# Expert weights in 16 KB rows, two ring slots to a matrix, on one core of a Trainium2 chip

## The chip, the cores and the metric

The kernel runs on one core of a Trainium2 chip (trn2). The metric is the device time of one execution, in microseconds (us). The kernel before takes 2732.53 us, the median of 3 runs (2731.9 to 2733.25).

## The reference: what is computed

A float32 network over 256 tokens of 1024 features. Its first part has two layers. Each layer scales and shifts its input by vectors made from a condition (the `ada` weights), mixes along the sequence (a gated convolution), adds and normalises, and runs a mixture of experts. Two more layers follow (`f1`, `hy`, `f2` in the kernel: feed-forward, attention, feed-forward), which the change does not touch. What matters here, from the reference:

```
def expert_block(args):
    xblk, e = args
    hid = jax.nn.silu(xblk @ w_gate[e]) * (xblk @ w_up[e])
    return hid @ w_down[e]
```

There are 32 experts to a layer. `w_gate[e]` and `w_up[e]` are 1024 x 512 and `w_down[e]` is 512 x 1024, so an expert has three matrices of 2 MB and a layer 192 MB, in float32. Each token goes to two experts of one group, by a router's scores.

## The kernel before, in words

**The ring.** All weights come through one ring in SBUF: `ring`, of `NSLOT` = 6 slots, each 128 partitions x 2048 float32 (8 KB to a partition, 1 MB in all). `wanted` lists what is needed in the order of use; from it the planner makes `pieces`, one to a slot: piece n goes to slot n % 6. `sync_engine` walks over the pieces in order, on the one queue of SP. Before it issues piece n it waits until piece n - 6 has been read (semaphore `ring_read`, line L734), then it issues the DMA at L738. The order of TensorE's steps is written out by hand in `moe`.

**An expert's pieces.** `want_experts` asks for four `up` pieces of expert e (gate and up weights of input features 0 to 511, then gate and up weights of 512 to 1023) and then for the two `down` pieces of expert e - 1 (inner features 0 to 255, then 256 to 511). That is six pieces, so each kind comes back to the same slots every time. Within a piece, partition p holds 4 whole rows of the gate or up matrix (input features 4p to 4p + 3 of that half), or 2 rows of the down matrix, side by side in memory: one run of 8 KB to a partition.

**TensorE in the stage of the experts.** For each e it runs `up(e)`, `down(e - 1)`, every second time `combine`, then `turn(e)` and, for the first 24, `gather` of later tokens. `up(e)` (matmul at L1096) has up to 64 gathered tokens as the stationary operand, 128 x 64, and the weights as the moving operand; the token block takes half of the array's columns, and so the inner features are cut in two halves c: c = 0 goes to PSUM partitions 0 to 63, c = 1 to 64 to 127, and both run beside each other. One matmul has 512 moving columns: 256 gate weights and 256 up weights of the same half and input chunk, from two neighbouring slots:

```
r4 = two.rearrange("p u (k n) -> p k u n", k=4)
ins = pe.matmul(b[64 * c:64 * c + 64, :], xg[:, u, kc, x0:x0 + CAP], r4[:, k, :, 256 * c:256 * c + 256],
                start=kc == 0, stop=kc == KC - 1)
```

There are 16 such matmuls to an expert in the program. A float32 matmul appears in the profile as two instructions, so an expert has 32 of them there. After the first 8 (the first half of the input features) two slots are given back, after the second 8 the next two. `down(e)` (L1115) has 8 matmuls and gives back one slot after each half.

**After `up`.** ScalarE takes silu of the gate half of the bank (L2491) and VectorE multiplies by the up half (L1961). Both use `by_two`, so that neighbouring inner features come apart (stride of two elements), because partition p of a down piece holds features 2p and 2p + 1. `turn` transposes the product for `down`.

**Around it.** `router_shift` (L804) moves the scale and shift columns of `ab` to the feature order that the gathered tokens have (4p + k within a half), by 16 small matmuls with `ident[:, k::4]` as the stationary operand. ScalarE copies the result (L2465). The tokens' high and low parts `vh` and `vl` are written by L2473 (ScalarE) and L1827 (VectorE) through `by_four`, which reads `vv` with a stride of four elements, 16 bytes. The gather evacuations L1931, L1940, L2453 and L2461 use the scale. For expert 0 the first half of gate and up and both down pieces are read early to places outside the ring (`early_loads`, L709).

## Time and profile before

| | |
|---|---|
| median of 3 runs | 2732.53 us |
| the profiled execution's own time | 2728.11 us |
| its span in the trace | 2726.3 us |
| mean granted TensorE clock | 0.983 of 2.4 GHz |
| TensorE matmuls busy | 2486.4 us, 91% |
| TensorE weight loads busy | 1839.1 us, 67% |
| VectorE, ScalarE, GpSimd busy | 1291.5, 863.6, 298.5 us |
| read from HBM | 709.72 MB, 261 GB/s over the span |
| DMA packets | 254197 |

Busy time is a union over the span: two matmuls that run beside each other count once. The duration of one instruction (mean ns) is then longer than busy time divided by count. The share of DMA is the mean over the core's 16 DMA engines; a stretch that is full reads 1.00 or 1.01.

### The profile page before, as it was taken

Reading aid. Unit: us, or ns where it says so; the run is one execution under the profiler, and the core shown is the slowest. Engines: PE = TensorE matmul, PEld = TensorE weight load, DVE = VectorE, ACT = ScalarE, POOL = GpSimd, SP = SyncE. Lnnn points to the kernel's source line nnn. Section 1 sums busy time; section 2 is a strip of 40 time slices with the busy share of each in tenths; the row PEclk is TensorE's granted clock in tenths of the full one; section 3 lists DMA queues with packets and bytes.
Section 4 is the critical chain, followed back from the end, with each engine's and each line's share of the span. In section 5 each row is a group of like instructions: output and inputs, shape, how many; then the busy total and the mean of one; then the engine's idle time right before and its main releaser. Section 6 shows DMA issues by size and latency. Waiting matters only on the chain.

```text
span 2726.3 us, 39201 instructions
## 1 busy us (share of the span) xinstructions
PE 2486.4 (91%) x15956; PEld 1839.1 (67%) x15957; DVE 1291.5 (47%) x2250; ACT 863.6 (32%) x1462; POOL 298.5 (11%) x382
## 2 busy tenths in 40 slices
PE   5899898988898988988899999989999999989998
PEld 3564433333694333333599888879989988888997
DVE  5454323221664332222454675565465467555545
ACT  2242111110332111110244444444444444444443
POOL 0210010000000010000000122330010011233001
PEclk9999999999998999999999999999999999999999
DMA  9988999999764999999765443335655544334372
GB/s 354 366 357 318 420 420 419 415 420 419 265 238 175 420 419 419 416 420 419 294 202 186 132 150 124 124 124 182 201 167 199 194 137 155 117 116 155 128 241 81
DMA packets 254197, 716.26 MB, mean 263 GB/s; under 512 B 14544, under 2 KB 171872, under 8 KB 197696
## 3 DMA queue, kind: packets, MB, share of 16 engines
q1 hardware_dynamic: 250336, 708.80, 69.0%
q0 software_dynamic: 1616, 2.45, 0.3%
q8 instruction: 129, 2.11, 0.3%
q10 hardware_dynamic: 2064, 2.47, 0.3%
q14 instruction: 52, 0.43, 0.0%
HBM read 709.72 MB, written 1.05 MB: 261 GB/s over the span
## 4 chain that ended last, share of the span: by engine, by line
PE 59%; DMA 22%; issue 7%; DVE 6%; POOL 3%; ACT 2%; SPq 1%; ACTq 0%; DVEq 0%; POOLq 0%
DMA ring<-in_e_w_up_dram 20%; PE w L837 17%; PE w L1096 10%; PE y L879 10%; PE w L841 9%; PE w L1115 2%; DMA ring<-in_ada_w_dram 2%; PE w L1372 2%; PE y L762 1%; POOL arena L2770 1%; PE w L1357 1%; PE y L1148 1%; DVE wsp L1481 1%; DMA xa<-in_x_dram 1%; SPq L738 1%
## 5 line engine op out<-in xcount | busy, mean ns | idle before, releaser
L1481 DVE TENSOR_TENSOR wsp<-ring,wsp 128x1024 fp32r<-128x1024 f32 x470 | 578.7, 1237 | 406.0 <-ACT wsp L1471 405.3
L837 PE MATMUL w<-hh,wsp 128*128 128x256 f32 x4832 | 638.4, 285 | 8.5 <-DVE wsp L1481 8.1
L837 PEld LDWEIGHTS w<-hh,wsp 128*128 128x128 f32 x4832 | 607.6, 192 | 28.9 <-issue 15.9
L1471 ACT CAST wsp<-ring 128x1024 fp32r<-128x1024 f32 x470 | 487.9, 1045 | 398.2 <-PE w L841 217.5
L1096 PE MATMUL w<-ring,arena 128*64 128x512 f32 x2016 | 459.8, 598 | 104.8 <-DMA ring<-in_e_w_up_dram 98.3
L1096 PEld LDWEIGHTS w<-ring,arena 128*64 128x64 f32 x2016 | 155.5, 137 | 374.6 <-issue 373.5
L841 PE MATMUL w<-hl,wsp 128*128 128x256 f32 x2416 | 339.1, 283 | 0.0
L841 PEld LDWEIGHTS w<-hl,wsp 128*128 128x128 f32 x2416 | 311.8, 192 | 0.0
L879 PE MATMUL y<-wsp,zsp 128*128 128x512 f32 x1104 | 267.2, 392 | 3.9 <-DVE wsp L1481 3.8
L2491 ACT ACTIVATE ht<-w 128x256 f32<-128x256 f32 x64 | 40.0, 625 | 700.4 <-PE w L1096 700.4
L1961 DVE TENSOR_TENSOR ht<-w,ht 128x256 f32<-128x256 f32 x64 | 39.5, 618 | 455.1 <-ACT ht L2491 455.1
L879 PEld LDWEIGHTS y<-wsp,zsp 128*128 128x128 f32 x1104 | 201.8, 188 | 44.5 <-DVE wsp L1481 6.1
L1115 PE MATMUL w<-ring,ht 128*64 128x512 f32 x992 | 225.1, 592 | 1.1 <-issue 1.1
L1115 PEld LDWEIGHTS w<-ring,ht 128*64 128x64 f32 x992 | 82.5, 137 | 130.7 <-issue 101.6
L1974 DVE TENSOR_TENSOR arena<-w,gb 64x512 f32<-64x512 f32 x128 | 88.2, 689 | 144.1 <-PE w L1115 142.1
L2696 POOL TENSOR_TENSOR zsp<-arena,zsp 128x256 fp32r<-128x256 f32 x92 | 69.2, 752 | 724.8 <-ACT zsp L2347 724.8
L2683 POOL TENSOR_TENSOR small<-small 128x1 f32<-128x1 f32 x20 | 16.2, 812 | 817.5 <-DVE small L1611 817.5
L2770 POOL TENSOR_SCALAR arena<-arena,small 128x128 f32<-128x128 f32 x96 | 62.1, 665 | 275.0 <-DVE small L2251 275.0
L2540 ACT ACTIVATE arena<-w 128x256 f32<-128x256 f32 x88 | 33.8, 384 | 144.9 <-PE w L841 144.9
L762 PE MATMUL y<-ring,arena 128*32 128x512 f32 x384 | 53.9, 679 | 22.6 <-DMA ring<-in_ada_w_dram 22.5
L879 PE MATMUL y<-wsp,hh 128*128 128x512 f32 x224 | 69.8, 393 | 4.9 <-DVE wsp L1481 3.4
L2080 DVE TENSOR_TENSOR arena<-w,arena 128x256 f32<-128x256 f32 x88 | 37.4, 425 | 77.8 <-ACT arena L2540 77.6
(341 smaller groups left out, 2478.3 us busy)
## 6 DMA issues: line engine op xcount, KB each, us to landing
ring<-in_e_w_gate_dram SPq DMA_DIRECT2D x126, 1024.0 KB, 8.6
ring<-in_e_w_up_dram SPq DMA_DIRECT2D x126, 1024.0 KB, 10.8
ring<-in_e_w_down_dram SPq DMA_DIRECT2D x124, 1024.0 KB, 12.2
ring<-in_ffn_in_dram SPq DMA_DIRECT2D x88, 1024.0 KB, 5.4
ring<-in_w_in_dram SPq DMA_DIRECT2D x50, 1024.0 KB, 5.2
ring<-in_ada_w_dram SPq DMA_DIRECT2D x48, 1024.0 KB, 12.6
ring<-in_ffn_out_dram SPq DMA_DIRECT2D x44, 1024.0 KB, 5.0
ring<-in_b_w_in_dram SPq DMA_DIRECT2D x12, 1024.0 KB, 8.9
```

Of the source, the lines that this page charges most:

```text
L762: ins = pe.matmul(ada_sum(l, cb)[32 * g:32 * g + 32, :], cact[:, kc, :], ring[:, n % NSLOT, g * 512:(g + 1) * 512], start=kc == 0, stop=kc ...
L837: pe.matmul(dst, a[:, kc * m:(kc + 1) * m], hh[:, kc, :], start=kc == 0 and j == 0, stop=False)
L841: ins = pe.matmul(dst, wh[:, kc * m:(kc + 1) * m], hl[:, kc, :], start=False, stop=kc == KC - 1)
L879: ins = pe.matmul(YB[2 * t + h][:, :], z[:, t * P:(t + 1) * P], a[:, h * 512:(h + 1) * 512], start=k == 0 and j == 0, stop=k == n - 1 and ...
L1096: ins = pe.matmul(b[64 * c:64 * c + 64, :], xg[:, u, kc, x0:x0 + CAP], r4[:, k, :, 256 * c:256 * c + 256], start=kc == 0, stop=kc == KC - 1)
L1115: ins = pe.matmul(b[64 * dh:64 * dh + 64, :], he[:, i, c, h, :], w[:, c, 512 * dh:512 * dh + 512], start=h == 0 and c == 0, stop=h == 1 an ...
L1372: ins = pe.matmul(b[:, T * c:T * c + T], a[:, k * 256 + c * P:k * 256 + c * P + P], z[:, k, :], start=k == 0 and j == 0, stop=k == 3 and j ...
L1471: ac.copy(shaped(halves(i)[0], u.shape), u.cut(ring[:, u.piece % NSLOT, :])).then_inc(*mark("w_high", i))
L1481: ve.tensor_tensor(shaped(lo, u.shape), u.cut(ring[:, u.piece % NSLOT, :]), shaped(hi, u.shape).bitcast(F32), ALU.subtract).then_inc(*mark ...
L1974: ve.tensor_tensor(ye[p0:p0 + 64, pr, dh, :], b[at_, :], gb[at_, 512 * dh:512 * dh + 512], ALU.mult).then_inc(*mark("ye", l, d_))
L2696: po.tensor_tensor(lo, src, hi.bitcast(F32), ALU.subtract).then_inc(*mark("z_lo", key, k))
L2770: ins = po.tensor_scalar(sm[:, 2 * u + q, a:z], sm[:, 2 * u + q, a:z], rd[:, k:k + 1], 0.5, ALU.mult, ALU.mult)
```

## The change

Gate, up and down matrices now come whole. A gate or up matrix is one DMA of 2 MB (`wide_piece`), partition p getting its 8 rows 8p to 8p + 7, 16 KB in one run, in two neighbouring slots; a down matrix likewise, 4 rows of 4 KB to a partition. Order: gate, up, then down of the expert before. Exceptions: expert 0's gate and up stay cut in two (rows 0 to 3 of each partition early, 4 to 7 through the ring, and the ring's half is now used first), and down of expert 31 stays in two pieces.

`up(e)` reads the gate matrix through first and gives its two slots back, then the up matrix. A matmul has 256 moving columns instead of 512, and there are 32 instead of 16. Inner feature 4q + 2c + j goes to half c, place j, q: the moving operand of a matmul is now read through `by_part`, with a step of four elements (16 bytes) between columns. The silu and the product need no `by_two` any more. A down matrix's two slots are given back together, after the second half of `down`.

For the new order of the input features (8p + k) `router_shift` gets 32 small matmuls instead of 16, with `twice` (two copies of the identity, made by VectorE) as its source; each writes both of two neighbouring features, and GpSimd picks one by a mask (two TENSOR_SCALAR and one TENSOR_TENSOR, 128 x 16) before the gather evacuations may run. `by_eight` reads `vv` with a stride of eight elements.

The diff, cut to its core:

```
@@ constants
+    for u in range(2):
+        c[:, C_ODD + u] = np.arange(P) // 16 % 2 == u
@@ want_experts
-                    wanted.extend(("up", l, e_, h) for h in range(4))
+                    wanted.extend(("up", l, e_, u) for u in range(2))
                 if e_ >= 1:
-                    wanted.extend(("down", l, e_ - 1, h) for h in range(2))
+                    wanted.append(("down", l, e_ - 1))
@@ pieces
+        def wide_piece(key, src):
+            n = len(pieces)
+            assert n % 2 == 0
+            piece_of[key] = n
+            pieces.append({"wide": src, "units": [], "read": n})
+            pieces.append({"units": [], "read": n})
...
-                src = I[("e_w_gate", "e_w_up")[u]][l, e_, 512 * g:512 * g + 512, :]
+                src = I[("e_w_gate", "e_w_up")[u]][l, e_].rearrange("(p k) n -> p k n", p=P)
...
-        def in_ring(key):
-            return ring[:, piece_of[key] % NSLOT, :]
+        def two_slots(s, k):
+            return ring[:, s:s + 2, :].rearrange("p u (k n) -> p (u k) n", k=k // 2)
...
-        def by_four(a):
-            return a.rearrange("p (g q k) -> p g k q", g=2, k=4)
+        def by_eight(a):
+            return a.rearrange("p (q k) -> p k q", k=KC)
-        def by_two(a):
-            return a.rearrange("p (q c) -> p q c", c=2)
+        def by_part(a):
+            return a.rearrange("p (q c j) -> p c j q", c=2, j=2)
@@ sync_engine
+                if "wide" in piece:
+                    slot_free(n - NSLOT)
+                    slot_free(n + 1 - NSLOT)
+                    sp.dma_start(two_slots(n % NSLOT, piece["wide"].shape[1]), piece["wide"]).then_inc(
+                        *mark(f"ring{n % NSLOT}", n, by=16))
@@ router_shift
-                o = WB[3][:, 64:80].rearrange("p (v g k) -> p v g k", v=2, g=2)
+                o = WB[3][:, 64:96].rearrange("p (v k b) -> p v k b", v=2, k=KC)
                 for j in range(4):
-                    for k in range(4):
-                        pe.matmul(o[32 * j:32 * j + 32, :, :, k], ident[:, k::4],
-                                  ab[:, 0:2, :].rearrange("p v (g j) -> p v g j", g=2)[:, :, :, j], start=True, stop=True)
+                    for k in range(KC):
+                        pe.matmul(o[32 * j:32 * j + 32, :, k, :], twice[:, k::KC],
+                                  ab[:, 0:2, 2 * j:2 * j + 2], start=True, stop=True)
@@ up(e_), e_ > 0
+                        for v in range(2):
+                            np_ = piece_of["up", l, e_, v]
+                            pe.wait_ge(*at(f"ring{np_ % NSLOT}", np_))
+                            w = two_slots(np_ % NSLOT, KC)
+                            for kc in range(KC):
+                                for c in range(2):
+                                    ins = pe.matmul(b[64 * c:64 * c + 64, T * v:T * v + T], x(kc), by_part(w[:, kc, :])[:, c],
+                                                    start=kc == 0, stop=kc == KC - 1)
                             ins.then_inc(*mark("ring_read", np_))
@@ vector_engine, the product
-                        ve.tensor_tensor(hd[:, i, :].rearrange("p (c q) -> p q c", c=2), by_two(b[:, T:2 * T]),
-                                         hd[:, i, :].rearrange("p (c q) -> p q c", c=2), ALU.mult).then_inc(*mark("hd", l, e_))
+                        ve.tensor_tensor(hd[:, i, :], b[:, T:2 * T], hd[:, i, :], ALU.mult).then_inc(*mark("hd", l, e_))
@@ scalar_engine, silu
-                        ac.activation(hd[:, i, :].rearrange("p (c q) -> p q c", c=2), by_two(bank_of(("up", e_))[:, 0:T]), ACT.Silu).then_inc(*mark("silu", l, e_))
+                        ac.activation(hd[:, i, :], bank_of(("up", e_))[:, 0:T], ACT.Silu).then_inc(*mark("silu", l, e_))
@@ pool_engine, moe
+                po.tensor_scalar(wide, cols[:, :, 0], const[:, C_ODD:C_ODD + 1], None, ALU.mult).then_inc(*mark("ones", "even", l))
+                po.tensor_scalar(odd_cols, cols[:, :, 1], const[:, C_ODD + 1:C_ODD + 2], None, ALU.mult).then_inc(*mark("ones", "odd", l))
+                po.wait_ge(*at("ones", "odd", l))
+                po.tensor_tensor(wide, wide, odd_cols, ALU.add).then_inc(*mark("ones", "scale", l))
```

How the instructions stand on SP's queue, in the middle of layer 0, where two short loads of norm vectors (`lnp`) stand between the down weights of one expert and the next expert's gate weights (each row: line, tensor written and read, shape; in brackets the semaphore it waits for). Before:

```order
L738 DMA ring<-in_e_w_down_dram 128x2048 [waits ring_read] x2
L725 DMA lnp<-in_ffn_ln_g_dram 128x1024 [waits x_new]
L725 DMA lnp<-in_ffn_ln_b_dram 128x1024
L738 DMA ring<-in_e_w_gate_dram 128x2048 [waits ring_read]
L738 DMA ring<-in_e_w_up_dram 128x2048 [waits ring_read]
L738 DMA ring<-in_e_w_gate_dram 128x2048 [waits ring_read]
L738 DMA ring<-in_e_w_up_dram 128x2048 [waits ring_read]
L738 DMA ring<-in_e_w_down_dram 128x2048 [waits ring_read] x2
```

And with the change:

```order
L754 DMA ring<-in_e_w_down_dram 128x4096 [waits ring_read]
L745 DMA lnp<-in_ffn_ln_g_dram 128x1024 [waits x_new]
L745 DMA lnp<-in_ffn_ln_b_dram 128x1024
L754 DMA ring<-in_e_w_gate_dram 128x4096 [waits ring_read]
L754 DMA ring<-in_e_w_up_dram 128x4096 [waits ring_read]
L754 DMA ring<-in_e_w_down_dram 128x4096 [waits ring_read]
```

Six DMAs of 1 MB to an expert have become three of 2 MB. The gate matrix stands whole ahead of the up matrix.

TensorE's queue for one expert, from its first weights to the transposes of `turn` (`w` is the PSUM bank, `arena` holds the gathered tokens, `ht` the inner features). Before:

```order
L1096 MATMUL w<-ring,arena 64x512 [waits ring1,ring0,ye]
L1096 MATMUL w<-ring,arena 64x512 x7
L1096 MATMUL w<-ring,arena 64x512 [waits ring3,ring2]
L1096 MATMUL w<-ring,arena 64x512 x7
L1115 MATMUL w<-ring,ht 64x512 [waits ring4,he]
L1115 MATMUL w<-ring,ht 64x512 x3
L1115 MATMUL w<-ring,ht 64x512 [waits ring5]
L1115 MATMUL w<-ring,ht 64x512 x3
```

And with the change:

```order
L1130 MATMUL w<-ring,arena 64x256 [waits ring0,ye]
L1130 MATMUL w<-ring,arena 64x256 x15
L1130 MATMUL w<-ring,arena 64x256 [waits ring2]
L1130 MATMUL w<-ring,arena 64x256 x15
L1149 MATMUL w<-ring,ht 64x512 [waits ring4,he]
L1149 MATMUL w<-ring,ht 64x512 x3
L1149 MATMUL w<-ring,ht 64x512 [waits ring4]
L1149 MATMUL w<-ring,ht 64x512 x3
```

The matmuls of `up` are twice as many and half as wide. They wait for one DMA at a time where they waited for two, of 2 MB in both cases. `down` keeps its matmuls, and both its halves wait for the same DMA.

## Rows read from the trace of the kernel before

**Rows 1.** The page's part 1: busy time, share of the span, instructions.
```profile
PE 2486.4 (91%) x15956; PEld 1839.1 (67%) x15957; DVE 1291.5 (47%) x2250; ACT 863.6 (32%) x1462; POOL 298.5 (11%) x382
```
**Rows 2.** Busy time by stretch; columns as in the first line; third stretch: feed-forward.
```profile
core 0: us, PE busy (x) PEld busy (x) DVE busy (x) ACT busy (x) POOL busy (x), PEclk, DMA share, GB/s
284.00:722.00 438.00, 379.65 (x1750) 168.87 (x1747) 123.85 (x208) 58.05 (x102) 11.42 (x7) 0.99 1.00 410
860.00:1325.00 465.00, 411.14 (x1888) 176.71 (x1884) 122.43 (x195) 52.94 (x90) 10.21 (x4) 1.00 1.01 416
1400.00:1500.00 100.00, 100.00 (x705) 94.11 (x705) 48.78 (x48) 45.72 (x61) 8.88 (x12) 1.00 0.67 223
```
**Rows 3.** The chain that ended last, two experts of layer 0: start, us, what.
```profile
599.92 3.67 PE w L1096 x16
603.60 0.33 SPq L738
603.98 10.78 DMA ring<-in_e_w_up_dram
614.88 3.67 PE w L1096 x16
```
**Rows 4.** Groups on TensorE: shapes, count, busy us, mean ns, idle before and releaser.
```profile
L1096 PE MATMUL w<-ring,arena 128*64 128x512 f32 x2016 | 459.8, 598 | 104.8 <-DMA ring<-in_e_w_up_dram 98.3 <-issue 3.2 <-DVE arena L1940 2.9
L1096 PE MATMUL w<-arena 128*64 128x512 f32 x32 | 7.3, 597 | 3.5 <-DVE arena L1931 3.5
L941 PE MATMUL w<-arena 128*32 128x256 f32 x144 | 8.8, 379 | 0.0
L837 PE MATMUL w<-hh,wsp 128*128 128x256 f32 x4800 | 634.0, 285 | 8.5 <-DVE wsp L1481 8.1 <-DVE vv L2196 0.4
```
**Rows 5.** SP's queue, one expert: start, us, DMA issued.
```profile
598.62 0.33 SPq L738 DMA_DIRECT2D ring<-in_e_w_gate_dram  x1
598.99 0.43 SPq L738 DMA_DIRECT2D ring<-in_e_w_up_dram  x1
603.60 0.33 SPq L738 DMA_DIRECT2D ring<-in_e_w_gate_dram  x1
603.98 0.43 SPq L738 DMA_DIRECT2D ring<-in_e_w_up_dram  x1
605.32 2.04 SPq L738 DMA_DIRECT2D ring<-in_e_w_down_dram  x2
613.79 0.33 SPq L738 DMA_DIRECT2D ring<-in_e_w_gate_dram  x1
```
**Rows 6.** Groups on ScalarE and VectorE, operands with and without a step.
```profile
L2509 ACT CAST hh<-arena 128x1024 fp32r<-128x1024 f32 x32 | 33.3, 1041 | 21.5 <-DVE arena L1974 21.5
L2473 ACT CAST zsp<-vv 128x1024 fp32r<-128x1024 f32 x4 | 8.2, 2048 | 0.0
L1481 DVE TENSOR_TENSOR wsp<-ring,wsp 128x1024 fp32r<-128x1024 f32 x468 | 577.2, 1239 | 406.0 <-ACT wsp L1471 405.3 <-issue 0.3
L1827 DVE TENSOR_TENSOR wsp<-vv,zsp 128x1024 fp32r<-128x1024 f32 x4 | 8.0, 1996 | 2.4 <-ACT zsp L2473 2.4
```
**Rows 7.** TensorE weight loads of 32 columns: ns min/median/max; contiguous, then stepped.
```profile
L762 PEld LDWEIGHTS y<-ring,arena x384: 106/110/177, 11.2 to 213.8; 128*32 128x32 f32 x192
L804 PEld LDWEIGHTS w<-ab,const x64: 134/156/158, 193.4 to 814.7; 128*32 128x32 f32 x64
```
**Rows 8.** Groups of silu and product, and the same without a step elsewhere.
```profile
L2491 ACT ACTIVATE ht<-w 128x256 f32<-128x256 f32 x64 | 40.0, 625 | 700.4 <-PE w L1096 700.4
L1961 DVE TENSOR_TENSOR ht<-w,ht 128x256 f32<-128x256 f32 x64 | 39.5, 618 | 455.1 <-ACT ht L2491 455.1
```
**Rows 9.** TensorE by time in layer 0, `router_shift`: start, us, instructions.
```profile
193.38 1.27 PE L804 MATMUL w<-ab,const 128*32 128x4 f32 x29
222.22 3.65 PE L1096 MATMUL w<-arena 128*64 128x512 f32 x16 [1.77 <-DVE arena L1931]
```

More of the change, by code:

```diff
@@ L39 @@
 NFIRST = 161
-NCONST = 2145
+C_ODD = 2145
+NCONST = 2147
 CAP = 64
@@ L313, in program @@
         var, rsd = small[:, 212:214], small[:, 214:216]
+        both_cols, odd_cols = small[:, 256:288], small[:, 288:304]
         uA = area(0, KC, 288)
@@ L565, in program @@
+                src = I[("e_w_gate", "e_w_up")[u]][l, e_].rearrange("(p k) n -> p k n", p=P)
+                assert e_ or len(pieces) % 2 == u
+                if e_ == 0:
+                    early[l].append((early_up[:, u, :], src[:, 0:4, :], "in_x"))
+                    piece_of[w] = len(pieces)
+                    pieces.append({"parts": [(lambda r: r, src[:, 4:8, :])], "units": [], "read": len(pieces) + 1 - u})
+                else:
+                    wide_piece(w, src)
             elif w[0] == "down":
-                _, l, e_, h = w
@@ L696, in late, with slot_free @@
                                     sp.sem_inc(s_, 1)
+            def slot_free(n):
+                if pieces[n]["units"]:
+                    for i in pieces[n]["units"]:
+                        sp.wait_ge(*low_done(i))
+                else:
+                    sp.wait_ge(*at("ring_read", pieces[n].get("read", n)))
             def early_loads(l):
@@ new lines, in up @@
+                    if e_ == 0:
+                        for v in range(2):
+                            np_ = piece_of["up", l, 0, v]
+                            pe.wait_ge(*at(f"ring{np_ % NSLOT}", np_))
+                        s0 = np_ % NSLOT - 1
+                        for h, two in ((1, ring[:, s0:s0 + 2, :]), (0, early_up)):
+                            if h == 0:
+                                pe.wait_ge(*at("in_x", "early", l))
+                            r4 = two.rearrange("p u (k q c j) -> p k c u j q", k=4, c=2, j=2)
+                            for k in range(4):
+                                for c in range(2):
+                                    o = b[64 * c:64 * c + 64, :].rearrange("p (u j q) -> p u j q", u=2, j=2)
+                                    ins = pe.matmul(o, x(4 * h + k), r4[:, k, c], start=(h, k) == (1, 0), stop=(h, k) == (0, 3))
+                            ins.then_inc(*(mark("ring_read", np_) if h else mark("ring_read", "early_up", l)))
+                    else:
+                        for v in range(2):
+                            np_ = piece_of["up", l, e_, v]
+                            pe.wait_ge(*at(f"ring{np_ % NSLOT}", np_))
+                            w = two_slots(np_ % NSLOT, KC)
+                            for kc in range(KC):
+                                for c in range(2):
+                                    ins = pe.matmul(b[64 * c:64 * c + 64, T * v:T * v + T], x(kc), by_part(w[:, kc, :])[:, c],
+                                                    start=kc == 0, stop=kc == KC - 1)
@@ L1111, in down @@
                             pe.wait_ge(*at(f"ring{np_ % NSLOT}", np_))
-                            w = ring[:, np_ % NSLOT, :].rearrange("p (k n) -> p k n", k=2)
-                        for c in range(2):
+                            s0 = (piece_of["down", l, e_, 0] + h) % NSLOT
+                            w = ring[:, s0, :].rearrange("p (k n) -> p k n", k=2)
+                        for j in range(2):
                             for dh in range(2):
-                                ins = pe.matmul(b[64 * dh:64 * dh + 64, :], he[:, i, c, h, :], w[:, c, 512 * dh:512 * dh + 512],
-                                                start=h == 0 and c == 0, stop=h == 1 and c == 1)
-                        if e_:
+                                ins = pe.matmul(b[64 * dh:64 * dh + 64, :], he[:, i, j, h, :], w[:, j, 512 * dh:512 * dh + 512],
+                                                start=h == 0 and j == 0, stop=h == 1 and j == 1)
+                        if e_ and (h == 1 or np_ != piece_of["down", l, e_, 1]):
                             ins.then_inc(*mark("ring_read", np_))
@@ L1928, in gathered_half @@
                     ve.wait_ge(*at("route_s", "row", l))
+                    ve.wait_ge(*at("ones", "scale", l))
                     for k in range(2):
@@ L2450, in gathered_half @@
                     ac.wait_ge(*at("route_s", "row", l))
+                    ac.wait_ge(*at("ones", "scale", l))
                     for k in range(2):
```

128 lines of the change are left out of this document (57 added, 71 removed).

## The prediction
> **What bounds the kernel now.** I began with the page's first part. TensorE is busy for 2486.4 of 2726.3 us [rows 1], but that is a mean over stages with different limits, so I read the stretches of the two layers' experts, the only ones the change touches in size. There the 16 DMA engines are full, share 1.00 and 1.01 at 410 and 416 GB/s, while TensorE is busy for 379.65 of 438 and 411.14 of 465 us, 87 and 88% [rows 2]. So these 903 us are bound by the transfers, and TensorE has some 12% to spare. The chain of waits shows one beat of this: 3.67 us of matmuls, 0.4 us on SP's queue, 10.78 us until the up weights have landed, and again; 614.88 - 599.92 = 14.96 us from expert to expert [rows 3]. An expert's weights are 6.29 MB, and 6.29 MB in 14.96 us are 420 GB/s. The reader should see that the 10.78 us is no latency but a queue: six transfers are out or in line at a time.
>
> TensorE's own cost of an expert: 14.96 x 0.88 = 13.1 us. Of it `up` takes (459.8 + 7.3) / 64 = 7.3 us [rows 4]. It waited 104.8 us ahead of `up` in all, nearly all of it for the up weights [rows 4]. That idle time is the whole cover for anything that makes matmuls dearer; past it, each microsecond counts in full.
>
> **The change, part by part.**
>
> *Rows of 16 KB.* 184 DMAs of 2 MB replace 368 of 1 MB (62 gate and up matrices and 30 down matrices to a layer). No row has a 16 KB transfer, so its price is bounded. Nothing gained is one end. For the other I estimate a fixed cost per row from two stretches: the experts' 8 KB rows move at 416/1.01 = 412 GB/s per unit of share, the feed-forward stretch, by the source's shapes two thirds 1 KB rows and one third 4 KB rows, at 223/0.67 = 333 [rows 2]. On 16 engines an 8 KB row then takes 318 ns, and 1 MB of the mixture 50.4 us of engine time; with a cost a per row and b per KB that solves to a of about 15 ns, b of about 38 ns. A 16 KB row would take 621 ns instead of 636, 2.4% off, at most 22 us of the 903. I take the middle, 11 us, for the case in which the transfers stay the bound.
>
> The Trainium skill (DMA: Bandwidth & Descriptors, Where 436 GB/s comes from) puts the fabric's ceiling at 435 GB/s. The same page's table (Measured) gives 341 GB/s for a DMA of 1 MB and 425 for 16 MB, by which doubling the DMA's size should pay a lot; the trace disagrees, 420 GB/s with 1 MB, since the queue is never empty. By the ceiling alone the gain would be at most 3.5% of 903, 31 us.
>
> *Twice as many matmuls, half as wide.* The streaming work is the same. What is added is the cost of one more pair. Where four column groups run beside each other at 256 columns, an instruction takes 8800/144 = 61 ns of busy time, a set of four 245 ns [rows 4], against 213 ns that 256 columns need at the pace of `up` (427 of its 2 x 228 = 456 ns for 512 columns; 427 is 512 columns at two cycles of 2.4 GHz). So 32 ns are overhead. An expert has 32 pairs now: 32 x 245 = 7.8 us, half a microsecond more, 35 us in all. As long as it is only this, it lies within the 104.8 us of idle time and costs nothing.
>
> *The moving operand with a step of 16 bytes.* Here I see the decision. Before, a matmul of `up` reads runs of 256 neighbouring weights. Now every column lies 16 bytes from the one before. No matmul of the kernel before has such a moving operand of any length, so this too is bounded by its neighbours. The lower end is nothing. Against it stand three engines' readers in this very trace. ScalarE casts 128 x 1024 in 1041 ns from neighbouring elements and in 2048 ns where it reads `vv` with a step of 16 bytes; VectorE's subtraction goes from 1239 to 1996 ns on the same operand [rows 6]. And TensorE's other operand: a weight load of 32 columns takes 106 ns at least without a step and 134 at least (156 at the median) with `ident[:, k::4]`, a step of 16 bytes [rows 7]. Per element that is +0.98, +0.74, and +0.88 ns (+1.44 at the medians). A matmul of `up` takes 427/512 = 0.83 ns for a column, so such a reader would about double it. What speaks for nothing: a float32 column stays in the array for two cycles, and at 256 columns the single-pass matmuls take 634.0/4800 us = 132 ns each, so the moving reader delivers at least 1.9 elements per ns from neighbouring addresses [rows 4], more than `up` asks of it per half. But there it passes over 16 bytes in 2 ns; with the step it would have to pass over 16 bytes in every 0.83 ns, faster than ScalarE (2048/1024 = 2 ns), VectorE or the weight loads do in their rows. I take the doubling.
>
> The Trainium skill (Advanced Engine Details and Errata, Memory Cachelines) says that SBUF has lines of 16 bytes and that at least two hits on a line are needed to hide the access, with a penalty otherwise. By that rule the step taken here, one hit to a line, is just past what is free. It speaks of engines in general and gives no factor; rows 6 agree with it for ScalarE and VectorE, and no row shows it for a moving operand.
>
> The sum: 64 experts x 32 pairs = 2048 pairs, each 2 x 213 + 32 = 459 ns, 940 us, for 467 us now: +473 us. The 104.8 us of idle time go: +368 us. An expert then takes 5.7 us longer, the transfers have a share near 0.7, and their rate no longer matters.
>
> *Slots.* Gate slots come back after half of `up`, up slots after the other half, as before. Both down slots now come back at the end of `down`, where the first came back some 1.8 us earlier. The queue covers it: the down DMAs are issued at 605.3 and 607.0, when the 2 MB issued at 603.6 and most of those of 598.6 are still in line (they land at 614.8), and nothing else is issued until 613.8 [rows 3, 5]. Zero.
>
> *Silu and product* lose their steps and perhaps 0.2 us each of 625 and 618 ns [rows 8]; TensorE runs `down(e - 1)` meanwhile. Zero.
>
> *`router_shift`* has 32 more instructions a layer at 1270/29 = 44 ns [rows 9], 1.4 us, 2.8 in all. GpSimd's three small operations (under a microsecond each) and VectorE's copy run while the router works, between 194 and 222 us [rows 9]: covered; without cover some 3 us a layer. I count +2.8 us.
>
> Sum: 2728.1 + 368 + 2.8 = 3099 us against the profiled execution's own time. The median of the runs is 4.4 us above that: **3104 us**. With +0.74 ns a column instead (VectorE's) a pair takes 435 ns, and the time is 3055; with +0.98 (ScalarE's) it is 3180; that case's own range is 3045 to 3230.
>
> **The rivals.**
>
> *The step is free.* The moving operand is read as fast as before, TensorE goes from 13.1 to 13.6 us an expert and the transfers stay the bound at 14.6 to 14.96. Then the time is 2732.5 - 11 + 2.8 = 2724 us, 2705 at best. For it: the moving reader is the fastest of all in rows 4, and it may fetch ahead. Against it: rows 6 and 7. This is the case on the other side.
>
> *Free, and no gain.* The 16 KB rows are cut into smaller packets, so the change doesn't do what it says, or the fixed cost per row is nil. 2730 to 2738 us. A packet count that has not fallen would show it.
>
> *Both halves share one reader.* The two matmuls of a pair then share the slowed rate: 4 x 213 + 32 = 884 ns a pair, 1810 us of `up`, +1343 - 105 + 3: 3974 us. Against it: four column groups stream 256 columns each in 245 ns [rows 4], so they are not served in turn now.
>
> *The queue runs dry behind the down slots.* It decides once less than 1.8 us of transfers are in line as `down` ends; 62 x 1.8 = +112 us, 2845. Rows 3 and 5 show over 7 us in line.
>
> **How the numbers follow.** The doubled read 0.51; free and gaining 0.32; free with nothing gained 0.08; the shared reader 0.05; the dry queue and other mishaps 0.04. Of the doubled case a little lies above 3230. Low end 2703, near the best of the free case, high end 3230: it leaves out the shared reader and the doubled case's upper tail, some 0.13. Cases of both signs hold most of the chance, so note that 3045 to 3230 is the likeliest one's range and that the middle between is nearly empty. 0.2% is about what a measurement of this kernel can tell from no change. Faster 0.32, the same 0.08, slower 0.60.
>
> **What would show it.** The group of `up`'s matmuls on TensorE: instructions of 256 columns with a mean well above the 379 ns of rows 4, and a busy time near 940 us rather than 500. DMA share in the experts near 0.7, not 1.0; no idle time ahead of `up` released by a transfer. The chain of waits there all TensorE. 23552 fewer packets, if rows are moved as 16 KB. If the group's busy time is below some 570 us, the central step is wrong and the time must come from the DMA rate: then 2705 to 2730 us, and GB/s above 416.

## The result, and the profile after

| | before | changed |
|---|---|---|
| median of the runs | 2732.89 us (2731.9 to 2733.51, 4 runs) | 3113.21 us (3108.41 to 3120.01, 4 runs) |
| span of the profiled execution | 2726.3 us | 3105.8 us |
| TensorE busy | 2486.4 us, 91% | 2966.9 us, 96% |
| `up` on TensorE, all groups | 467.1 us | 941.1 us |
| idle time ahead of `up` in the ring | 104.8 us | 8.0 us |
| share of the DMA engines in layer 0's experts | 1.00 | 0.79 |
| packets on SP's queue | 250336 | 223840 |

The changed kernel takes 1.140 times as long, 95% interval 1.1385 to 1.1414. Slower, as forecast: 3104 us were predicted, within 2703 to 3230.

The same view as [rows 1], from the page of the changed kernel (busy time, share of the span, instructions of each engine):

```profile
PE 2966.9 (96%) x18004; PEld 2007.1 (65%) x18005; DVE 1280.2 (41%) x2252; ACT 848.6 (27%) x1462; POOL 302.0 (10%) x388
```

TensorE gains 480.5 us of busy time, and the span grows by 379.5. The first stretch of [rows 2], layer 0's experts, of the changed kernel (same columns: busy time and instructions of PE, PEld, DVE, ACT, POOL; granted clock; DMA share; GB/s):

```profile
284.00:722.00 438.00, 434.96 (x1962) 177.02 (x1960) 86.22 (x146) 35.65 (x68) 10.43 (x4) 1.00 0.79 302
```

The two bounds have changed places. Before, the transfers had a share of 1.00 and TensorE 87%; now TensorE has 99% and the transfers 0.79, at 302 GB/s instead of 410. The granted clock was 1.00 in the stretch, the 2.4 GHz level, and 0.99 before, so the extra time does not come from the clock.

TensorE's groups after, to set beside [rows 4] (shapes, count, busy us, mean ns, idle before and its releaser; L1130 is `up` from the ring; L1121 are its early parts of expert 0, and L1149 is `down`):

```profile
L1130 PE MATMUL w<-ring,arena 128*64 128x256 f32 x3968 | 911.5, 632 | 8.0 <-issue 8.0
L1149 PE MATMUL w<-ring,ht 128*64 128x512 f32 x992 | 224.8, 594 | 1.1 <-issue 1.1
L1121 PE MATMUL w<-arena 128*64 128x512 f32 x32 | 14.8, 1078 | 0.0
L1121 PE MATMUL w<-ring,arena 128*64 128x512 f32 x32 | 14.8, 1078 | 3.5 <-DVE arena L1971 3.5
```

`up` costs 911.5 + 14.8 + 14.8 = 941.1 us for the same multiplications that took 467.1, and no transfer releases any of it any more. `down`, whose operand kept its neighbours, takes 594 ns a matmul, 592 before. L1121 is the cleanest row: instructions of 512 columns as before, 597 ns before, 1078 now. What differs is the order in which the moving operand is read.

The chain that ended last, for one expert and a part of the next, as in [rows 3] (start us, us, what):

```profile
608.25 14.63 PE w L1130 x64
622.89 3.44 PE w L1149 x16
626.32 0.37 PE w L1161 x2
626.69 0.17 PE w L1170 x2
626.86 0.50 PE w L1172 x4
627.36 0.94 PE w L1095 x4
628.30 14.63 PE w L1130 x64
```

From this expert to the next it is now 628.30 - 608.25 = 20.05 us, where the expert of [rows 3] took 14.96, and TensorE holds every link. The 10.78 us wait for the up weights has gone from the chain. The 64 instructions are 32 pairs, one instruction for each half: 14.63 us by 32 is 457 ns a pair.

Silu and product, beside [rows 8], got shorter by 240 and 193 ns, on engines that wait for TensorE anyway (same columns as [rows 8]):

```profile
L2001 DVE TENSOR_TENSOR ht<-w,ht 128x256 f32<-128x256 f32 x64 | 27.2, 425 | 814.8 <-ACT ht L2530 814.8
L2530 ACT ACTIVATE ht<-w 128x256 f32<-128x256 f32 x64 | 24.6, 385 | 1082.7 <-PE w L1130 1053.2
```

### The profile page after: what moved, and what is told of

It is laid out like the page before. It is cut to its first block, busy times and chain, and to the rows that moved or that the text cites. A ratio compares the mean times of both kernels' runs of the same rounds, so it can differ in the third digit from the quotient of the medians.

```text
span 3105.8 us, 43240 instructions
## 1 busy us (share of the span) xinstructions
PE 2966.9 (96%) x18004; PEld 2007.1 (65%) x18005; DVE 1280.2 (41%) x2252; ACT 848.6 (27%) x1462; POOL 302.0 (10%) x388
## 3 DMA queue, kind: packets, MB, share of 16 engines
q1 hardware_dynamic: 223840, 708.79, 62.7%
## 4 chain that ended last, share of the span: by engine, by line
PE 84%; issue 5%; DVE 4%; DMA 2%; POOL 2%; ACT 2%; ACTq 0%; SPq 0%; DVEq 0%; POOLq 0%
PE w L1130 29%; PE w L862 16%; PE y L904 9%; PE w L866 8%; PE w L1149 7%; PE y L1182 2%; DMA ring<-in_ada_w_dram 1%; PE w L1095 1%; PE w L1407 1%; PE w L1121 1%; PE y L787 1%; PE w L1392 1%; POOL arena L2817 1%; DVE wsp L1516 1%; DMA xa<-in_x_dram 1%
## 5 line engine op out<-in xcount | busy, mean ns | idle before, releaser
L1130 PE MATMUL w<-ring,arena 128*64 128x256 f32 x3968 | 911.5, 632 | 8.0 <-issue 8.0
L1130 PEld LDWEIGHTS w<-ring,arena 128*64 128x64 f32 x3968 | 322.0, 154 | 558.2 <-issue 556.3
L2001 DVE TENSOR_TENSOR ht<-w,ht 128x256 f32<-128x256 f32 x64 | 27.2, 425 | 814.8 <-ACT ht L2530 814.8
L2530 ACT ACTIVATE ht<-w 128x256 f32<-128x256 f32 x64 | 24.6, 385 | 1082.7 <-PE w L1130 1053.2
L1149 PE MATMUL w<-ring,ht 128*64 128x512 f32 x992 | 224.8, 594 | 1.1 <-issue 1.1
L1149 PEld LDWEIGHTS w<-ring,ht 128*64 128x64 f32 x992 | 75.1, 141 | 140.8 <-issue 140.8
L1407 PE MATMUL w<-zsp,wsp 128*128 128x256 f32 x576 | 71.5, 284 | 3.0 <-DVE zsp L2250 3.0
L1407 PEld LDWEIGHTS w<-zsp,wsp 128*128 128x128 f32 x576 | 69.6, 192 | 6.2 <-issue 6.2
```

Source lines behind the costliest of these rows:

```text
L1130: ins = pe.matmul(b[64 * c:64 * c + 64, T * v:T * v + T], x(kc), by_part(w[:, kc, :])[:, c], start=kc == 0, stop=kc == KC - 1)
L1149: ins = pe.matmul(b[64 * dh:64 * dh + 64, :], he[:, i, j, h, :], w[:, j, 512 * dh:512 * dh + 512], start=h == 0 and j == 0, stop=h == 1 an ...
L1407: ins = pe.matmul(b[:, T * c:T * c + T], a[:, k * 256 + c * P:k * 256 + c * P + P], z[:, k, :], start=k == 0 and j == 0, stop=k == 3 and j ...
```

## The experiments

Ratios are to the kernel before, run beside each version on the same chip. Where one run alone was made, no interval is given. "A pair" is always two instructions of 256 columns in the profile, one for each half; its price is the group's busy time by half the count (where the instructions have 512 columns, half of that again). a, b, j and so on are the versions by the first letter of their labels.

### Is it the step? The same kernel, neighbouring columns

```diff
@@ up(e_), after
-    ins = pe.matmul(b[64 * c:64 * c + 64, T * v:T * v + T], x(kc), by_part(w[:, kc, :])[:, c],
+    ins = pe.matmul(b[64 * c:64 * c + 64, T * v:T * v + T], x(kc), w[:, kc, T * c:T * c + T],
```

(and the same for expert 0's early part).

> The changed kernel, but each matmul of `up` reads 256 neighbouring weights (features 256c to 256c + 255 for half c) instead of every fourth; the inner features then meet the wrong rows of the down matrix, all else is the change's. Theory 1 (the 16-byte step is the cost): the matmuls of `up` fall from 911 us busy to 470 to 500 us (pairs of about 245 ns), the transfers bound the experts again, 2710 to 2735 us. Rival (twice as many, narrower matmuls and their weight loads, or the new slot order, are the cost): 911 us busy stays, about 3110 us. The same run shows what 16 KB rows are worth: DMA at 420 GB/s if nothing (2733 to 2738 us), up to 430 if a fixed cost per row is saved (2710 to 2722 us).

Measured: 2748.62 us (2742.27 to 2756.37, 4 runs), 1.0074 times before, 1.0053 to 1.0094. The groups of `up` and of `down` on TensorE, columns as above:

```profile
L1130 PE MATMUL w<-ring,arena 128*64 128x256 f32 x3968 | 451.9, 382 | 38.6 <-DMA ring<-in_e_w_up_dram 27.3 <-issue 6.1 <-DMA ring<-in_e_w_gate_dram 5.1
L1149 PE MATMUL w<-ring,ht 128*64 128x512 f32 x992 | 226.2, 596 | 64.7 <-DMA ring<-in_e_w_down_dram 63.5 <-issue 1.1
```

911.5 us become 451.9, and the time falls by 365 us. Nearly all of the loss was the step. The size of the rest was not as expected: `up` is below the 470 to 500 us, the time above the 2710 to 2735. Two things stand out. A pair costs 451.9/1984 = 228 ns, exactly half of the 456 ns of the 512-column pair: cutting the matmuls in two costs nothing. And the kernel is still 0.7% slower than before; TensorE now waits most for **down** weights, 63.5 us, where before it waited for up weights.

### The step alone, in the kernel before

```diff
@@ up(e_), before
-    ins = pe.matmul(b[64 * c:64 * c + 64, :], xg[:, u, kc, x0:x0 + CAP], r4[:, k, :, 256 * c:256 * c + 256],
+    ins = pe.matmul(b[64 * c:64 * c + 64, :].rearrange("p (u j q) -> p u j q", u=2, j=2), xg[:, u, kc, x0:x0 + CAP],
+                    r4[:, k].rearrange("p u (q c j) -> p c u j q", c=2, j=2)[:, c],
```

> The kernel before with one edit: its matmuls of `up` (512 columns, 8 KB rows, old order of pieces) read each half's columns with the change's 16-byte step; the inner features meet the wrong rows of the down matrix. Theory 1: 1024 pairs of 2 x 427 + 32 ns, about 900 us busy for 460 now, less the idle time it uses up: 3070 to 3110 us. Rival (narrow matmuls, slot order): `up` stays at 460 us busy and the time at 2733 us.

Measured: 3101.6 us, one run. The group of `up` from the ring:

```profile
L1096 PE MATMUL w<-ring,arena 128*64 128x512 f32 x2016 | 920.5, 1080 | 8.0 <-issue 8.0
```

With 8 KB rows, wide matmuls, the old slots and the old shift, the step by itself brings 372 us (the kernel before, beside it, took 2729.99 us). 920.5/1008 = 913 ns a pair of 512 columns, 457 for 256. So the parts do not have to come together: one of them does it.

### Keeping the change's order of features, with a step of two elements inside

```diff
@@ by_part, and the order of the output
-            return a.rearrange("p (q c j) -> p c j q", c=2, j=2)
+            return a.rearrange("p (q c j) -> p c q j", c=2, j=2)
@@ silu and product read and write through by_two again, as before
```

The moving operand now reads two neighbours and skips two: both halves of every 16 bytes are used.

> The change, but the moving operand takes features 4q + 2c and 4q + 2c + 1 one after the other: two neighbours (8 bytes), then 8 bytes left out; silu and product put them apart as in the kernel before. Same result as the reference. If the price hangs on 16 bytes being passed over for each single column (about 1.67 ns for 16 bytes), two columns to 16 bytes take the 0.83 ns each that float32 needs anyway: `up` 470 to 500 us busy, 2710 to 2735 us. If every gap between addresses costs, `up` lies between 600 and 911 us busy and the time between 2800 and 3110 us.

Measured: 2747.46 us (2746.02 to 2749.13, 4 runs), 1.0058 times before, 1.0041 to 1.0075. TensorE's groups:

```profile
L1134 PE MATMUL w<-ring,arena 128*64 128x256 f32 x3968 | 472.5, 391 | 36.1 <-DMA ring<-in_e_w_up_dram 23.4 <-DMA ring<-in_e_w_gate_dram 6.6 <-issue 6.1
L1153 PE MATMUL w<-ring,ht 128*64 128x512 f32 x992 | 226.2, 596 | 51.3 <-DMA ring<-in_e_w_down_dram 50.0 <-issue 1.1
```

238 ns a pair. It recovers 366 of the 380 us with the change's layout in memory; the 2710 to 2735 us expected were missed, as in a. The feature order that the down weights want was never the trouble; the order in which a matmul walks through it was.

### How the price depends on the step

```diff
@@ up(e_), before, 8 bytes
-    r4[:, k, :, 256 * c:256 * c + 256],
+    r4[:, k, :, c::2],
@@ up(e_), after, 12 bytes (::3), and in another kernel 32 bytes (::8)
-    by_part(w[:, kc, :])[:, c],
+    flat[:, min(kc * 512 + c, 2 * SLOT - 3 * (T - 1) - 1):][:, ::3][:, 0:T],
```

> The kernel before, its matmuls of `up` reading every second weight (step 8 bytes, features 2q + c; wrong ones for the down matrix). Two columns come from each 16 bytes at 0.83 ns a column, 16 bytes in 1.67 ns. If pairs were free because of that and not because the two were neighbours: 460 us busy, 2733 us. If only real neighbours are free: 600 us busy or more, 2780 us or more.

> The changed kernel with the moving operand of `up` (experts 1 to 31) read with a step of 3 elements, 12 bytes, from the same two slots; the columns are then not the right ones. If the price is set by how fast 16 bytes are passed over, a column costs 12/16 of the stepped one: with 1.78 ns for a column at 16 bytes (457 ns for 256), 1.34 ns, 343 ns a pair, some 680 us busy for 3968 instructions and a time of 2850 to 2880 us. If a column is free as long as its step is below 16 bytes: 450 to 480 us busy and about 2745 us. If any step costs as 16 bytes do: 911 us busy, 3110 us.

> The same with a step of 8 elements, 32 bytes. If a column's price is one access to memory however far the next is (what I expect), nothing changes against 16 bytes: 911 us busy, about 3110 us. If it grows with the distance: about 1820 us busy, time about 4000 us.

Measured, one run each (the kernel before beside them, one run too: 2738.8 us): 2734.37, 2883.88 and 3110.95 us. Each is the first case of its expectation, 12 bytes 4 us above its range. One line of TensorE's groups from each, first the kernel before with 8 bytes, then the changed kernel with 12, then with 32:

```profile
L1096 PE MATMUL w<-ring,arena 128*64 128x512 f32 x2016 | 484.2, 623 | 86.5 <-DMA ring<-in_e_w_up_dram 80.4 <-issue 6.1
```

```profile
L1130 PE MATMUL w<-ring,arena 128*64 128x256 f32 x3968 | 691.8, 513 | 8.6 <-issue 7.0 <-DVE arena L1980 1.0 <-DMA ring<-in_e_w_gate_dram 0.6
```

```profile
L1130 PE MATMUL w<-ring,arena 128*64 128x256 f32 x3968 | 925.6, 640 | 8.0 <-issue 8.0
```

| step | columns to 16 bytes | ns a pair of 256 | ns a column |
|---|---|---|---|
| 4 bytes (neighbours) | 4 | 228 | 0.89 |
| pairs, 16 bytes apart | 2 | 238 | 0.93 |
| 8 bytes | 2 | 240 | 0.94 |
| 12 bytes | 1.33 | 349 | 1.36 |
| 16 bytes | 1 | 457 to 459 | 1.79 |
| 32 bytes | 1 | 467 | 1.82 |

The price follows how many stretches of 16 bytes the operand goes through, and does not grow with the distance. At 12 bytes 256 columns go through 192 of them: 349/192 = 1.82 ns each; at 16 and 32 bytes through 256, 1.79 and 1.82 ns each. At 8 bytes it is 128, 1.8 x 128 = 230 ns, about what the columns take anyway, so the step is nearly free. Steps above 32 bytes and other types than float32 were not run. The Trainium skill (Advanced Engine Details and Errata, Memory Cachelines) wants at least two hits on a line of 16 bytes; for this moving operand the table agrees at both sides of that limit, 240 ns with two hits and 457 with one.

In the kernel before, a step of 8 bytes is hidden: the group is 24.4 us dearer than in [rows 4] and the idle time ahead of it falls from 104.8 to 86.5 us. The cover worked as read from [rows 4].

### Do the two halves share a reader?

```diff
@@ up(e_), after: the halves one after the other
-    for kc in range(KC):
-        for c in range(2):
+    for c in range(2):
+        for kc in range(KC):
```

and the same with neighbouring columns.

> The change, with the loop over the two halves c outside the loop over input chunks: 8 matmuls of one half, then 8 of the other, so that two matmuls that could run beside each other are no longer neighbours. Theory 1a (each stream is slowed to half its rate, both still run beside each other in the changed kernel): an instruction now takes some 440 to 460 ns alone, 29 us an expert in `up`, about 1850 us busy, time about 4050 us. Theory 1b (the step does not slow a stream, it only keeps the two halves from running beside each other, 213 ns each in turn): nothing is left to lose, `up` stays at about 911 us and the time at about 3110 us.

> Control for the run with the halves in turn: 8 matmuls of one half, then 8 of the other, all reading neighbouring weights (wrong features for the down matrix). If two halves stream side by side when they are neighbours in the queue and one alone keeps its own pace, an instruction takes 213 to 230 ns here (256 columns at 0.83 ns), about 880 us busy, time about 3080 us. If neighbouring reads let even one half go faster than that, the time is nearer 2750 us.

Measured, one run each: 3683.15 us with the step, 2926.66 us with neighbours. The group of `up`, with the step and then with neighbours:

```profile
L1130 PE MATMUL w<-ring,arena 128*64 128x256 f32 x3968 | 1478.8, 633 | 8.0 <-issue 8.0
```

```profile
L1130 PE MATMUL w<-ring,arena 128*64 128x256 f32 x3968 | 719.4, 382 | 8.6 <-issue 8.0 <-DMA ring<-in_e_w_gate_dram 0.6
```

Neither time was the one expected, but the pace of a single half was. Two stretches of TensorE's timeline, each inside a series of one half (start us, us, instructions), with the step and then with neighbours:

```profile
612.05 5.16 PE L1130 MATMUL w<-ring,arena 128*64 128x256 f32 x11
```

```profile
536.39 2.11 PE L1130 MATMUL w<-ring,arena 128*64 128x256 f32 x9
```

Less the last instruction's own 0.63 and 0.38 us, that is (5.16 - 0.63)/10 = 453 ns from start to start with the step, and (2.11 - 0.38)/8 = 216 ns with neighbours. One half alone takes as long as the two do side by side, 457 and 228 ns a pair. So the halves do not share a reader: each pays for its own stretches of 16 bytes, and the second half is free when it runs beside the first.

The times missed because the series overlap where they meet. Here `up` (L1130) ends and `down` (L1149) begins, in the version with the step:

```profile
604.23 0.64 PE L1149 MATMUL w<-ring,ht 128*64 128x512 f32 x1
604.68 0.64 PE L1130 MATMUL w<-ring,arena 128*64 128x256 f32 x1
604.71 0.59 PE L1149 MATMUL w<-ring,ht 128*64 128x512 f32 x1
605.14 0.64 PE L1130 MATMUL w<-ring,arena 128*64 128x256 f32 x1
605.14 0.64 PE L1149 MATMUL w<-ring,ht 128*64 128x512 f32 x1
605.61 0.64 PE L1130 MATMUL w<-ring,arena 128*64 128x256 f32 x1
```

The next series uses the other half of the columns and starts while the last instructions of the one before are still to come. Between the series of `up` it is the same: at each of the three seams of an expert four pairs start within 20 ns of each other (57 with neighbours). Of 64 instructions 12 are thus hidden, and 52 x 453 ns = 23.6 us, for 1478.8/62 = 23.9 measured; with neighbours 52 x 216 ns = 11.2 us, for 11.6.

### What is left: the down weights and their slots

b, with the down weights in two DMAs of 1 MB (rows of 8 KB), whose slots come back half by half as before:

```diff
@@ pieces
-                elif e_ < E - 1:
-                    wide_piece((*w, 0), src)
-                    piece_of[*w, 1] = piece_of[*w, 0]
```

> The run with pairs (step-free streaming, right result), but every down matrix in two DMAs of 1 MB with rows of 8 KB, each slot given back after its half of `down`. If the late release of the down slots leaves the transfers short of work (TensorE waited 50 us for down weights in the run with pairs, none before): 4 to 12 us less than its 2747 us, 2735 to 2743 us, with those waits gone. If it costs nothing, as I had put down: 2747 us.

Measured: 2740.22 us (12 runs), 1.0029 times before, 1.0019 to 1.0039. TensorE's groups:

```profile
L1131 PE MATMUL w<-ring,arena 128*64 128x256 f32 x3968 | 475.4, 391 | 79.1 <-DMA ring<-in_e_w_up_dram 42.2 <-DMA ring<-in_e_w_gate_dram 30.6 <-issue 6.1
L1150 PE MATMUL w<-ring,ht 128*64 128x512 f32 x992 | 224.4, 592 | 1.8 <-issue 1.1 <-DMA ring<-in_e_w_down_dram 0.6
```

The wait for down weights goes from 50.0 to 0.6 us; most of it returns ahead of gate and up, which is what happens when transfers are the bound. The gain is 7 to 9 us (7 by the two medians, 9 by what each has above the kernel before beside it), 1.0058 to 1.0029, with intervals that don't meet. It shows most in a window behind `add_residual`, 3.6 us of further matmuls between two experts. The same 10 us of the kernel before, then of b, then of j (columns as in [rows 2]):

```profile
500.00:510.00 10.00, 9.41 (x48) 3.85 (x46) 3.64 (x5) 2.33 (x5) 0.00 (x0) 1.00 1.01 421
```

```profile
500.00:510.00 10.00, 10.00 (x78) 5.63 (x78) 1.76 (x3) 0.63 (x1) 0.00 (x0) 1.00 0.75 288
```

```profile
500.00:510.00 10.00, 10.00 (x76) 5.26 (x73) 1.17 (x2) 0.63 (x1) 0.00 (x0) 1.00 0.88 339
```

Where TensorE has a longer piece of work, slots come back late and the queue does run dry: share 0.75 with both down slots returned together, 0.88 with one after the other. (The kernel before has its own dip 10 us earlier, 0.96 from 490 to 500 us.) But it is not only there. Two of b's long stretches of experts, one in each layer:

```profile
290.00:480.00 190.00, 172.79 (x1171) 96.91 (x1168) 55.98 (x95) 23.30 (x38) 10.34 (x4) 1.00 1.00 419
1130.00:1300.00 170.00, 154.07 (x1058) 86.27 (x1058) 37.54 (x55) 17.96 (x32) 0.00 (x0) 1.00 0.98 413
```

In four such stretches (290 to 480, 600 to 690, 890 to 1030 and 1130 to 1300 us) b has shares of 0.98 to 1.00 and 413 to 419 GB/s, j 1.01 and 423 to 424. So with down matrices whole the queue is short of work in ordinary experts too, by a little. j changes three things at once, the return of the slots, the landing in two parts and down's rows of 8 KB; the runs do not part them, but the missing share in b points to slots that come back late.

### Rows of 16 KB

The same number of 2 MB DMAs, each as two runs of 8 KB to a partition:

```diff
@@ wide pieces
-                    wide_piece(w, src)
+                    wide_piece(w, I[("e_w_gate", "e_w_up")[u]][l, e_].rearrange("(h p k) n -> p h (k n)", h=2, p=P))
...
-                    sp.dma_start(two_slots(n % NSLOT, piece["wide"].shape[1]), piece["wide"]).then_inc(
+                    sp.dma_start(ring[:, n % NSLOT:n % NSLOT + 2, :], piece["wide"]).then_inc(
```

Once on a, down weights too (first text), and once on j (second).

> The run with neighbouring reads (a_neighbours) with its 2 MB DMAs made of two runs of 8 KB to a partition instead of one of 16 KB: same sizes, same order, same slots, only the row is half as long (the token features then meet other weights). If a row has a fixed cost of about 15 ns: the rate in the experts falls by up to 2.4%, 10 to 22 us more than a_neighbours' 2748 us. If 16 KB rows are worth nothing: the same 2748 us within 3 us.

> The run with down in halves (j_down_halves), its gate and up DMAs of 2 MB made of two runs of 8 KB to a partition instead of one of 16 KB; slots, order and matmuls are the same, the token features meet other weights. There the transfers bound the experts without a gap, so the rate tells the row length's worth. If 16 KB rows are what lifts the rate from 420 (kernel before) to 424 GB/s in that run: 418 to 421 GB/s here between 290 and 480 us, and 5 to 10 us more than its 2740 us. If not (DMA size or chance): 424 GB/s and 2740 us.

Measured: k 2755.37 us (6 runs), 1.0083 (1.0067 to 1.0099), against a's 1.0074 (1.0053 to 1.0094): not told apart by the times; k lies 5 to 7 us higher, where 10 to 22 or none were expected. l 2746.64 us (5 runs), 1.0054 (1.0038 to 1.0069), against j's 1.0029 (1.0019 to 1.0039): the intervals overlap by a hair; 6 us more than j and the rate are as the first case expected. A full stretch of layer 0's experts shows more than the times do; before, then j, then l (columns as in [rows 2]):

```profile
290.00:480.00 190.00, 165.09 (x758) 70.84 (x758) 56.50 (x95) 24.69 (x40) 10.21 (x4) 1.00 1.01 420
```

```profile
290.00:480.00 190.00, 172.79 (x1173) 98.14 (x1171) 57.26 (x97) 24.92 (x42) 10.36 (x4) 1.00 1.01 424
```

```profile
290.00:480.00 190.00, 171.48 (x1148) 97.40 (x1146) 57.27 (x97) 24.75 (x42) 10.35 (x4) 0.99 1.01 418
```

All three have a share of 1.01. In four such stretches over both layers before moves 419 to 420 GB/s, j (16 KB rows for gate and up) 423 to 424, and l (8 KB runs) 414 to 419. So in j the 16 KB rows of gate and up give about 1% over before, as estimated, and a DMA of 2 MB in runs of 8 KB gives nothing or a little less than nothing. k against a says the same of the row: 411 to 418 GB/s against 417 to 421. But a and b, with all three matrices whole as in the change, move 413 to 421 GB/s, on average no more than the kernel before; as it seems, the late slots take there what the rows give.

### `router_shift` twice

```diff
@@ router_shift, before
-                for j in range(4):
+                for j in [0, 1, 2, 3] * 2:
```

> The kernel before with router_shift's 16 small matmuls issued twice (32 instructions more to a layer), nothing else. The run with neighbouring reads began its experts 6.0 us later than the kernel before in layer 0 and is 0.7% slower than it, though its stream of up is as fast. If the doubled router_shift is what delays it: 2 to 6 us a layer, 2737 to 2745 us. If it costs what I put down (44 ns an instruction, 1.4 us a layer): 2733 us, hardly to be told from no change; then the delay comes from something else at that place (the masks on GpSimd, the order of the ring).

Measured: 2734.7 us (12 runs), 1.0014 times before, 1.0004 to 1.0023: 1 to 6 us by the interval and 2.6 by the medians (2732.14 before), where 2.8 were priced. Neither case of the expectation, 2737 to 2745 or 2733 us, was met. TensorE by time (start, us, instructions), i, and then the changed kernel:

```profile
198.76 2.33 PE L804 MATMUL w<-ab,const 128*32 128x4 f32 x61
```

```profile
196.11 3.26 PE L829 MATMUL w<-ab,ht 128*32 128x4 f32 x61
```

61 of them take 2.33 us in i, 38 ns each, and 3.26 us in the changed kernel, 53 ns each, against 44 in [rows 9]. What differs is both operands, where the stationary one lies and the order of `ab`'s columns, and how the output is laid out. That part is not taken further.

## Why the prediction was right

**What bounds the kernel, and the cover.** Right. [Rows 2, 4] gave 104.8 us of idle time ahead of `up` as the whole cover. Now it is 8.0, and the kernel with a step of 8 bytes showed the cover at work.

**The step of 16 bytes.** Right, and nearly in size: 459 ns a pair were predicted, 457 to 459 measured, 940 us against 941.1. It had a chance of 0.51, hardly more than even, and the range of 2703 to 3230 us held a faster kernel as well as a slower one; what was right is the point forecast and its mechanism. The sum for TensorE: `up` +474.0 us, less 104.8 - 8.0 = 96.8 us of idle time, makes +377 of the span's 379.5. The step alone in the kernel before gave +372, and taking it away gave 365 back. The argument by neighbours held: the weight loads, ScalarE and VectorE [rows 6, 7] pay too, and the 2048/1024 = 2.0 ns of ScalarE stand beside TensorE's 1.8 ns. The argument for a free step, that the reader gets 1.9 elements per ns from neighbouring addresses [rows 4], does not carry over: what is limited is how many stretches of 16 bytes are gone through in a time.

**The working of 459 ns.** It was 2 x 213 + 32, and here two errors cancelled, by luck. Without a step a narrow pair was put at 213 + 32 = 245 ns; it takes 228 (a), 17 less, so that the +35 us for narrower matmuls do not exist in this loop: 451.9 us for the ring's group, less than before. The row the 32 ns were taken from, 245 ns for a set of four in a group of only 144 matmuls, was the wrong neighbour. The step was to add 213 ns to a pair; it adds 457 - 228 = 229, 16 more, because it doubles all of the pair. The sum was right to 0.5%.

**16 KB rows.** Off the path in the changed kernel, as put, since its share is 0.79 (near 0.7 was expected; the rate fell as expected, 302/410 = 0.74). The packets fell by 26496: the 23552 predicted, and 16 small ones for each of the 184 DMAs saved. Where transfers do bound, the gain in rate is about 1% in j, the size of the 1.2% taken, though my ends (0 to 2.4%) were wide, and nothing in a and b.

**Slots.** Zero was right for the change as made, since its transfers do not bind. The reason given was not general: with the step repaired, whole down matrices cost 7 to 9 us (b against j). The row I argued from [rows 3, 5] was one expert; behind the long stretches the queue has no 7 us in line, and over full stretches of experts a little is missing as well. The rival's +112 us was far too much.

**Silu and product.** -240 and -193 ns, in idle time. Right.

**`router_shift`.** 2.8 us were counted. Its added instructions take 3.26 - 1.27 = 2.0 us a layer, 4 in all, and between its start and the first `up` TensorE needs 31.8 us in layer 0 where it needed 28.8, 30.5 in layer 1 where it needed 30.3: 3.2 us in all. The doubling in the kernel before costs 1 to 6 us. So 2.8 was about right. GpSimd's masks and VectorE's copy are covered, as put.

**The rival "the step is free".** This had 0.32, at 2724 us, and it would have been wrong even with a free step: a, with neighbours in everything else like the change, takes 2748.62 us, 18.6 above before and not 8 below. In the spans, a is 13.3 us longer: some 4.3 and 2.9 us between `router_shift` and the first `up` of the two layers, and 3.8 and 1.1 us in the two stretches of experts (484.3 and 481.1 us against 480.5 and 480.0). Both were priced at about zero. The second holds the late down weights. The first is only in part the shift: in i, which has the doubled shift alone, the same two stretches are 1.0 us longer and 0.5 us shorter than before. The changed kernel has a's shift and masks, and in layer 1 takes 30.5 us where a takes 33.2, at a granted clock of 0.72 over the stretch against 0.59; the kernel before has 0.66. So the clock has a part in it, and what set it is open.

The small gain in rate of 16 KB rows does not pay for this, and with the slots mended (j) the time is still 0.29% above before. In j's trace the two stretches of experts take no longer than before; 2.9 and 2.7 us are added between `router_shift` and the first `up`. No version with the change's rows beats the kernel before; why j is not 9 us faster from its rate, but 8 us slower, is known only in part.

## What to carry to other kernels

Before a data layout is changed so that another operation may read in order, look at how the matmul's moving operand then goes through memory: in float32 it paid about 1.8 ns for each stretch of 16 bytes it touched, so two elements from each were as good as free and one doubled the matmul. The choice of which index varies fastest inside the same set of columns was worth 366 us here, with the same layout in memory. Two matmuls on two halves of the columns did not slow each other, with the step or without; issued half by half they lost most of that. And a cover found in one expert (slots, idle time) is to be looked for over whole stretches, and where the regular beat is interrupted.

## What was not expected of the hardware

Halving the width of the matmuls of two column halves cost nothing: 228 ns a pair of 256 columns, 456 a pair of 512.

TensorE does not start its matmuls strictly in the order of the queue: the first instruction of `down` started at 604.23 us, 1.4 us ahead of the last one of `up`, which stands before it and uses the other half of the columns. Four instructions of a series overlapped the next series so.

In the changed kernel a longer time at the lower clock follows `router_shift`. Granted clock over the same 14 us, behind the shift of layer 0, of the kernel before, then of the changed kernel (columns as in [rows 2]; the clock stands before the DMA share):

```profile
206.00:220.00 14.00, 12.44 (x80) 7.70 (x81) 12.13 (x68) 3.57 (x11) 0.00 (x0) 0.79 0.95 349
```

```profile
206.00:220.00 14.00, 14.00 (x70) 9.22 (x73) 10.43 (x57) 6.29 (x10) 0.00 (x0) 0.56 0.73 282
```

0.79 is a mix of the two levels; 0.56 means 1.2 GHz for most of it (0.50 throughout 210 to 220 us). Both kernels run the same work here, the router and the first tokens' moves. The changed kernel had 64 instructions of four columns ahead of it, the kernel before 32. In i, which also has 64 but of the old form, it is 0.76 over the same window (its shift is 2.6 us later), with 0.50 from 212 to 218 us. That more of these short matmuls alone draw the lower clock is thus not shown; the doubled shift in i moved the dip and did not lengthen it. The longer dip of the changed kernel may be part of the 3 us by which its first `up` is later; its cause stays open.

The transfers reached 424 GB/s in DMAs of 2 MB with 16 KB to a partition, and 414 to 419 GB/s in DMAs of the same size with two runs of 8 KB; the DMAs of 1 MB before had 419 to 420. At 2 MB the length of the row counts; the larger DMA alone gave no gain.
